# Expert layer of a two-block kernel: units in pairs, loads of half the rows of two units, gate and up products of 512 columns

## The chip, the cores and the metric

The kernel runs on one core of a Trainium2 chip. The metric is the device time of one execution in microseconds (us). Three executions of the kernel before are shown, with their median. Engines are named as the profile names them: PE is TensorE, DVE is VectorE, ACT is ScalarE, POOL is GpSimd, SP is SyncE, and PEld is PE's loading of weights.

## What is computed

The reference runs a first block of two layers (SwiGLU networks, attention with a linear recurrence, a short convolution) and a second block of two layers (a mixer each, then a dense network and a layer of experts) over 256 tokens of 1024 columns. The change touches the last part alone, the layer of 8 experts with 2 chosen per token. Every expert has a hidden width of 3584:

```python
def _swiglu(x, w_gate, w_up, w_down):
    return (jax.nn.silu(x @ w_gate) * (x @ w_up)) @ w_down

def _moe_swiglu(x, w_router, b_router, w_gate, w_up, w_down):
    logits = (x @ w_router).astype(jnp.float32) + b_router.astype(jnp.float32)
    top_vals, top_idx = lax.top_k(logits, TOP_K)
    top_w = jax.nn.softmax(top_vals, axis=-1)
    combine = jnp.sum(jax.nn.one_hot(top_idx, N_EXPERTS, dtype=jnp.float32) * top_w[..., None], axis=-2)
    out = jnp.zeros_like(x)
    for e in range(N_EXPERTS):
        out = out + combine[..., e:e + 1].astype(x.dtype) * _swiglu(x, w_gate[e], w_up[e], w_down[e])
    return out
```

## The kernel before

**Units.** All weights stream from HBM once. The gate and up weights of 128 hidden columns are one unit: 1 MB in `w_gu`, 128 rows of 8 KB, each row holding gate (8 blocks `k` of 128 columns) and then up (8 blocks). The down weights of the same 128 hidden columns are 0.5 MB in `w_d`, 128 rows of 4 KB. An expert has NF2 = 28 units, the layer 224. `N0` is the number of the layer's first unit.

**Exactness.** Every product of fp32 is made of three in the fp32r type: a value is split in hi (`wh_gu`, `wh_d`, a copy by ACT) and lo (`wl_gu`, `wl_d`, a subtraction by DVE), and `mm3` (L1719) issues hi x hi, hi x lo and lo x hi; these are the lines L1721, L1722 and L1723, whoever calls it.

**One expert.** Up to 128 tokens of an expert are gathered into slots by products with a one-hot matrix (`gather`, L2209, 16 products of 128 columns for each half), modulated by ACT (L741), and split in hi and lo (`XGH`, `XGL`, shown as mixT_hi and mixT_lo). For unit i PE runs `slot_gate_up` (L2256 on): the slots are the stationary operand, and for each of 8 blocks k the moving operand is `wh_gu[:, :, k, :]`, 128 gate columns and 128 up columns, so 24 products of 256 columns into half of a PSUM bank, `PB[:, n % 2, 0:256]`. ACT takes the silu of 128 columns (L758), DVE multiplies with the up half (L1457), PE transposes the result (`h_transpose`, L2269), ACT and DVE split it (L764, L1463), and `slot_down` issues 6 products of 512 columns into two banks in which the expert's sum grows. At an expert's end ACT evicts that sum, and PE adds it to the tokens by `scatter_previous` (L2225) some units into the next expert.

**Order.** It is written out by hand for each engine, in steps i of one unit:

- PE: gate and up of i, transpose of i - 1, down of i - 2.
- ACT: silu of i, hi of h of i - 1, hi of the gate and up weights of i + 2 (`moe_hi_gu`, L726), hi of the down weights of i (`moe_hi_d`, L733).
- DVE: gated product of i, lo of h of i - 1, lo of the down weights of i - 1 (`moe_lo_d`, L1444), lo of the gate and up weights of i + 2 (`moe_lo_gu`, L1439).
- SP: the load of gate and up weights of unit i (`load_moe_gu`, L358), then of the down weights of i - 3 (L366), into four buffers each (`RAW_GU`, `RAW_D`; two of them are shown as scratch). A load waits until DVE has made the lo of the unit four before.

hi and lo tiles have two buffers: the hi of unit n waits until PE has used unit n - 2. Two more units of gate and up weights than the layer has (`NU = START[-1] + 2`) are loaded and split at the end and not used. The steps are unrolled but for loops of four steps (`Fori`), which run twice. A second pass for an expert with more than 128 tokens stands behind a branch on the number `most_members` and is not entered with these inputs.

## Time and profile before

| | us |
|---|---|
| median of 3 runs | 2753.35 |
| lowest and highest of them | 2750.55, 2759.77 |
| profiled execution, span from the first to the last instruction | 2747.2 |
| PE busy in it | 2600.3 |
| PEld, DVE, ACT, POOL busy | 2379.0, 2165.5, 1483.6, 947.8 |
| expert layer in it, from routing to the last product | about 1680 to 2730 |

The profiled execution's time is shown by its span; the three runs were timed without a profile and lie 3 to 12 us above it. A row of the timeline gives a start, a duration, engine, line, operation, and what is written from what, by the names of tiles. Durations of matmuls overlap, since their ends are modelled: the distance of two starts is what a product costs. "Idle before" names what a wait ended with. In the tables of windows, PEclk is the granted clock of PE as a share of 2.4 GHz and the DMA share is the mean busy share of 16 DMA engines.

### The profile page before, as it was taken

Reading aid. Unit: us, or ns where it says so; the run is one execution under the profiler, and the core shown is the slowest. Engines: PE = TensorE matmul, PEld = TensorE weight load, DVE = VectorE, ACT = ScalarE, POOL = GpSimd, SP = SyncE. Lnnn points to the kernel's source line nnn. Section 1 sums busy time; section 2 is a strip of 40 time slices with the busy share of each in tenths; the row PEclk is TensorE's granted clock in tenths of the full one; section 3 lists DMA queues with packets and bytes.
Section 4 is the critical chain, followed back from the end, with each engine's and each line's share of the span. In section 5 each row is a group of like instructions: output and inputs, shape, how many; then the busy total and the mean of one; then the engine's idle time right before and its main releaser. Section 6 shows DMA issues by size and latency. Waiting matters only on the chain. (4 is left out here: it accounts for less than half of the span.)

```text
span 2747.2 us, 47482 instructions
## 1 busy us (share of the span) xinstructions
PE 2600.3 (95%) x17802; PEld 2379.0 (87%) x17802; DVE 2165.5 (79%) x2488; ACT 1483.6 (54%) x1930; POOL 947.8 (34%) x586
## 2 busy tenths in 40 slices
PE   8999899999998998888998978999999999999997
PEld 7999699999897998658998747999999999999986
DVE  5667666766787676987855997898989898989888
ACT  4337543443434334424334515777777777777765
POOL 6990089688789992126900130000000000000000
PEclk9999999999999998999999988999999999999999
DMA  8664267566566653324553415999999999999985
GB/s 309 252 237 148 103 241 256 202 250 254 191 241 229 220 183 134 115 105 164 183 184 138 164 63 192 343 350 333 352 335 349 338 347 343 347 345 346 340 320 216
DMA packets 129209, 670.58 MB, mean 244 GB/s; under 512 B 14672, under 2 KB 14992, under 8 KB 80064
## 3 DMA queue, kind: packets, MB, share of 16 engines
q1 hardware_dynamic: 111024, 604.72, 59.9%
q0 software_dynamic: 18064, 64.21, 6.9%
q8 instruction: 81, 1.33, 0.2%
q14 instruction: 40, 0.33, 0.0%
HBM read 667.82 MB, written 1.05 MB: 243 GB/s over the span
## 5 line engine op out<-in xcount | busy, mean ns | idle before, releaser
L1721 PE MATMUL work<-xT_hi,wh_gu 128*128 128x256 f32 x2088 | 593.9, 284 | 21.6 <-DVE xT_lo L985 12.0
L1722 PE MATMUL work<-xT_lo,wh_gu 128*128 128x256 f32 x2088 | 592.3, 284 | 0.0
L1723 PE MATMUL work<-xT_hi,wl_gu 128*128 128x256 f32 x2088 | 591.7, 283 | 0.0
L1721 PE MATMUL work<-wh_gu,mixT_hi 128*128 128x256 f32 x1792 | 507.5, 283 | 2.8 <-DVE wl_gu L1439 1.5
L1722 PE MATMUL work<-wl_gu,mixT_hi 128*128 128x256 f32 x1792 | 505.8, 282 | 0.0
L1723 PE MATMUL work<-wh_gu,mixT_lo 128*128 128x256 f32 x1792 | 505.5, 282 | 0.0
L857 DVE TENSOR_TENSOR wl_gu<-raw_gu,wh_gu 128x2048 fp32r<-128x2048 f32 x158 | 392.3, 2483 | 72.0 <-ACT wh_gu L395 71.5
L1721 PEld LDWEIGHTS work<-xT_hi,wh_gu 128*128 128x128 f32 x2088 | 401.3, 192 | 30.1 <-issue 21.3
L1722 PEld LDWEIGHTS work<-xT_lo,wh_gu 128*128 128x128 f32 x2088 | 401.7, 192 | 4.8
L1723 PEld LDWEIGHTS work<-xT_hi,wl_gu 128*128 128x128 f32 x2088 | 401.5, 192 | 0.0
L862 DVE TENSOR_TENSOR wl_d<-raw_d,wh_d 128x1024 fp32r<-128x1024 f32 x157 | 250.2, 1594 | 189.6 <-ACT wh_d L402 189.5
L1721 PE MATMUL acc<-wh_d,h_hi 128*128 128x512 f32 x912 | 380.4, 417 | 2.8 <-DVE wl_d L1444 2.7
L1723 PE MATMUL acc<-wh_d,h_lo 128*128 128x512 f32 x912 | 361.2, 396 | 0.0
L1722 PE MATMUL acc<-wl_d,h_hi 128*128 128x512 f32 x912 | 361.1, 396 | 0.0
L1721 PEld LDWEIGHTS work<-wh_gu,mixT_hi 128*128 128x128 f32 x1792 | 340.9, 190 | 12.5 <-DVE wl_gu L1439 1.7
L1722 PEld LDWEIGHTS work<-wl_gu,mixT_hi 128*128 128x128 f32 x1792 | 341.6, 191 | 8.8
L1723 PEld LDWEIGHTS work<-wh_gu,mixT_lo 128*128 128x128 f32 x1792 | 341.5, 191 | 0.0
L402 ACT ACTIVATE wh_d<-raw_d 128x1024 fp32r<-128x1024 f32 x157 | 166.2, 1059 | 276.1 <-PE acc L1723 276.1
L395 ACT ACTIVATE wh_gu<-raw_gu 128x2048 fp32r<-128x2048 f32 x158 | 300.7, 1903 | 25.4 <-PE acc L1723 25.0
L1652 POOL TENSOR_SCALAR scratch<-scratch,small 128x1024 f32<-128x1024 f32 x84 | 312.9, 3724 | 4.2
L1439 DVE TENSOR_TENSOR wl_gu<-raw_gu,wh_gu 128x2048 fp32r<-128x2048 f32 x113 | 259.1, 2293 | 38.0 <-ACT wh_gu L726 37.9
L1439 DVE TENSOR_TENSOR wl_gu<-scratch,wh_gu 128x2048 fp32r<-128x2048 f32 x112 | 256.6, 2291 | 25.5 <-ACT wh_gu L726 25.0
(436 smaller groups left out, 4785.6 us busy)
## 6 DMA issues: line engine op xcount, KB each, us to landing
raw_gu<-in_w_gu SPq DMA_DIRECT2D x271, 1024.0 KB, 5.2
raw_d<-in_w_d SPq DMA_DIRECT2D x269, 512.0 KB, 5.4
scratch<-in_w_gu SPq DMA_DIRECT2D x112, 1024.0 KB, 7.2
scratch<-in_w_d SPq DMA_DIRECT2D x112, 512.0 KB, 7.8
scratch<-in_w_mod POOLq DMA_DIRECT2D x96, 512.0 KB, 3.7
scratch<-in_s_b POOLq DMA_DIRECT2D x16, 256.0 KB, 2.9
rows<-in_norm_post POOLq DMA_DIRECT2D x6, 512.0 KB, 4.4
rows<-in_ln_g POOLq DMA_DIRECT2D x4, 512.0 KB, 5.5
```

What stands on the lines that cost most here:

```text
L395: act.activation(wh_gu[k][:, :, :, :].rearrange("p a k n -> p (a k n)"), raw_gu[k][:, :], ACT.Copy).then_inc(gu_hi, 1)
L402: act.activation(wh_d[k][:, :], raw_d[k][:, :], ACT.Copy).then_inc(d_hi, 1)
L857: TT(wl, raw_gu[k][:, :], wh.bitcast(F32), ALU.subtract).then_inc(gu_lo, 1)
L862: TT(wl_d[k][:, :], raw_d[k][:, :], wh_d[k][:, :].bitcast(F32), ALU.subtract).then_inc(d_lo, 1)
L1439: TT(wl, RAW_GU[k] if k > 1 else RAW_GU[k][:, :], wh.bitcast(F32), ALU.subtract).then_inc(gu_lo, 1)
L1652: link(pool.tensor_scalar(MW[n % 3], MW[n % 3], c, None, ALU.mult))
L1721: pe.matmul(out_, w[0], m[0], start=start, stop=False)
L1722: pe.matmul(out_, w[0], m[1], start=False, stop=False)
L1723: return pe.matmul(out_, w[1], m[0], start=False, stop=stop)
```

## The change

Two units 2p and 2p + 1 are a pair. Their two loads of gate and up weights no longer bring one unit each: load h brings, for both units, the blocks k of half h (4h to 4h + 3), so a row of the buffer has four pieces of 2 KB (gate of either unit, up of either unit) from four places of `w_gu`. A product then takes one block k with the gate columns of both units and the up columns of both, 512 columns in four pieces of 128, into a whole bank: 12 products per load, the first load opening the sum and the second closing it. Silu, gated product and the split of h work on 256 columns once per pair; the two transposes of a pair stand together; down of a unit comes in step i + 3 instead of i + 2, hi of its weights in step i + 1, lo in step i + 2. The two surplus units go. The unrolled part of an expert is 20 steps, the looped part 2 x 4; in the last expert ACT and DVE have no loop.

```diff
-NU = START[-1] + 2
+NU = START[-1]
...
+            pairs_gu = A["w_gu"][N0:N0 + NE * NF2].rearrange("(q u) p (g h c) -> q h p g u c", u=2, g=2, h=2)
+
+            def pieces(raw):
+                return raw.rearrange("p (g u c) -> p g u c", g=2, u=2)
...
-                sp.dma_start(RAW_GU[k] if k > 1 else RAW_GU[k][:, :], A["w_gu"][dyn + n]).then_inc(gu_landed4[k], 16)
+                sp.dma_start(pieces(RAW_GU[k] if k > 1 else RAW_GU[k][:, :]),
+                             pairs_gu[pair + i // 2, i % 2]).then_inc(gu_landed4[k], 16)
...
-            for i in range(NE * NF2, NE * NF2 + 3):
-                if i < NE * NF2 + 2:
-                    load_moe_gu(i)
-                load_moe_d(i - LATER)
+            for i in range(NE * NF2 - LATER, NE * NF2):
+                load_moe_d(i)
...
-                def step(i, at, e=0):
-
-                    silu(i, at, P)
-                    if i or e:
-                        h_hi(i - 1, at)
-                    moe_hi_gu(i + 2, at)
-                    if i == 1 and e:
+                def step(i, at, pairs, e=0, more=True):
+
+                    if i % 2:
+                        silu(i // 2, at)
+                    elif i or e:
+                        h_hi(i // 2 - 1, pairs)
+                    if more:
+                        moe_hi_gu(i + 2, at)
+                    if i == 2 and e:
                         act.wait_ge(d_used, N0 + at)
                         act.activation(YS, tile2(PA[:, 0:2, :]), ACT.Copy, scale=slot_share).then_inc(moe_s["y"], 1)
-                    moe_hi_d(i, at)
-                    if i == 2 and e:
+                    if i or e:
+                        moe_hi_d(i - 1, at)
+                    if i == 3 and e:
                         y_hi(e)
...
+                moe_hi_d(NF2 - 1, at)
+                h_hi(NPAIR - 1, pairs)
...
-                def step(i, at, e=0):
-
-                    gated(i, at, P)
-                    if i or e:
-                        h_lo(i - 1, at, PA[:, 2 + (N0 + i - 1) % 2, 0:P], P)
-                        moe_lo_d(i - 1, at)
-                    moe_lo_gu(i + 2, at)
+                def step(i, at, pairs, e=0, more=True):
+
+                    if i % 2:
+                        gated(i // 2, pairs)
+                    elif i or e:
+                        h_lo(i // 2 - 1, pairs)
+                    if i > 1 or e:
+                        moe_lo_d(i - 2, at)
+                    if more:
+                        moe_lo_gu(i + 2, at)
...
+                moe_lo_d(NF2 - 2, at)
                 moe_lo_d(NF2 - 1, at)
+                h_lo(NPAIR - 1, pairs)
...
+                def part_product(out_, xg, k, w, kk, start, stop):
+
+                    wh, wl = (x[:, :, :, :].rearrange("p g (u k) n -> p (g u) k n", u=2)[:, :, kk, :] for x in w)
+                    return mm3(out_, (XGH[xg][:, k, :], XGL[xg][:, k, :]), (wh, wl), start, stop)
+
+                def slot_gate_up(i, at, xg):
+
+                    n, half = N0 + i, i % 2
                     pe.wait_ge(gu_lo, at + (n + 1))
-                    for k in range(KD):
...
+                    for kk in range(4):
+                        last = part_product(PB[:, i // 2 % 2, :], xg, 4 * half + kk, (wh_gu[n % 2], wl_gu[n % 2]), kk,
+                                            half == 0 and kk == 0, half == 1 and kk == 3)
                     last.then_inc(gu_used, 1)
...
+                def step(i, at, pairs, e, xg):
+
+                    if i < 2:
+                        pe.wait_ge(moe_s["xg_l"], 2 * e + i + 1)
+                    slot_gate_up(i, at, xg)
+                    if i % 2 == 0 and (i or e):
+                        h_transpose(i // 2 - 1, pairs)
+                    if i == 3 and e:
+                        pe.wait_ge(moe_s["y"], e)
+                    if i >= 3 or e:
+                        slot_down(i - 3, at, pairs, i == 3, i == 2)
...
+                slot_down(NF2 - 3, at, pairs)
+                h_transpose(NPAIR - 1, pairs)
+                slot_down(NF2 - 2, at, pairs)
+                slot_down(NF2 - 1, at, pairs, stop=True)
```

The pass behind the branch is changed in the same way. Three places show how the instructions move. First PE, at the border from a unit's gate and up products (work<-...) to the transpose (acc<-const,scratch) and the down products (acc<-wh_d,...), in a step of the last expert. Before:

```order
L1721 MATMUL work<-wh_gu,mixT_hi 128x256
L1722 MATMUL work<-wl_gu,mixT_hi 128x256
L1723 MATMUL work<-wh_gu,mixT_lo 128x256
L2268 REGISTER_ALU
L2269 MATMUL acc<-const,scratch 128x128
L2274 REGISTER_ALU
L1721 MATMUL acc<-wh_d,h_hi 128x512
L1722 MATMUL acc<-wl_d,h_hi 128x512
L1723 MATMUL acc<-wh_d,h_lo 128x512
```

and with the change, in an even step:

```order
L1733 MATMUL work<-wh_gu,mixT_hi 128x512
L1734 MATMUL work<-wl_gu,mixT_hi 128x512
L1735 MATMUL work<-wh_gu,mixT_lo 128x512
L2283 REGISTER_ALU
L2285 MATMUL acc<-const,scratch 128x128 x2
L2290 REGISTER_ALU
L1733 MATMUL acc<-wh_d,h_hi 128x512
```

The three rows of a block k stand eight times in a unit before and four times in a step now; they are twice as wide, and an even step has two transposes, an odd one none. Second DVE at the end of the last expert: lo of the weights (wl_gu, wl_d), the gated product (scratch<-scratch,work) and lo of h. Before:

```order
L1457 TENSOR_TENSOR scratch<-scratch,work 128x128
L1463 TENSOR_TENSOR h_lo<-acc,h_hi 128x128
L1444 TENSOR_TENSOR wl_d<-scratch,wh_d 128x1024
L1439 TENSOR_TENSOR wl_gu<-raw_gu,wh_gu 128x2048
L1463 TENSOR_TENSOR h_lo<-acc,h_hi 128x128
L1444 TENSOR_TENSOR wl_d<-scratch,wh_d 128x1024
```

and with the change:

```order
L1473 TENSOR_TENSOR h_lo<-acc,h_hi 128x256
L1456 TENSOR_TENSOR wl_d<-raw_d,wh_d 128x1024
L1468 TENSOR_TENSOR scratch<-scratch,work 128x256
L1456 TENSOR_TENSOR wl_d<-raw_d,wh_d 128x1024
L1456 TENSOR_TENSOR wl_d<-scratch,wh_d 128x1024 x2
L1473 TENSOR_TENSOR h_lo<-acc,h_hi 128x256
```

The last wl_gu is gone, and the last h_lo, which stood ahead of the last wl_d, stands behind the last three of them. Third SP, the loads at the head of the layer's loop, with the change:

```order
L364 DMA raw_gu<-in_w_gu 128x4x512
L373 DMA raw_d<-in_w_d 128x1024
L364 DMA raw_gu<-in_w_gu 128x4x512
L373 DMA scratch<-in_w_d 128x1024
L364 DMA scratch<-in_w_gu 128x4x512
```

Their order and number per unit are as before; a row of a gate and up load, 128x2048 before, is now four runs of 512 columns.

## Rows read from the trace of the kernel before

**Rows 1.** The page: its first line and the engines' busy times.

```profile
span 2747.2 us, 47482 instructions
...
PE 2600.3 (95%) x17802; PEld 2379.0 (87%) x17802; DVE 2165.5 (79%) x2488; ACT 1483.6 (54%) x1930; POOL 947.8 (34%) x586
```

**Rows 2.** Windows over the expert layer (their columns are the first line here).

```profile
core 0: us, PE busy (x) PEld busy (x) DVE busy (x) ACT busy (x) POOL busy (x), PEclk, DMA share, GB/s
...
1965.00:2090.00 125.00, 125.00 (x890) 117.16 (x890) 111.24 (x120) 91.75 (x122) 0.00 (x0) 1.00 0.93 343
```

**Rows 3.** The chain of waits from 2000 to 2030 us, by line.

```profile
by line: PE work L1722 21.1%; PE work L1721 21.1%; PE work L1723 21.1%; PE acc L1723 10.1%; PE acc L1722 10.1%; PE acc L1721 9.2%; PE work L2209 5.9%; PE acc L2269 2.2%
```

**Rows 4.** Timeline of PE: start us, us, engine, line, operation, out<-in.

```profile
2000.10 0.28 PE L1721 MATMUL work<-wh_gu,mixT_hi 128*128 128x256 f32 x1
...
2002.85 0.28 PE L1723 MATMUL work<-wh_gu,mixT_lo 128*128 128x256 f32 x1
...
2003.31 0.39 PE L1722 MATMUL acc<-wl_d,h_hi 128*128 128x512 f32 x1
...
2004.47 0.28 PE L1721 MATMUL work<-wh_gu,mixT_hi 128*128 128x256 f32 x1
```

**Rows 5.** Pieces of the chain of waits in the mixer before: start us, us.

```profile
1648.13 0.23 PE acc L1721
...
1652.92 0.23 PE acc L1721
```

**Rows 6.** Timelines of ACT, DVE and SP's queue, one unit of the layer.

```profile
2003.16 0.28 ACT L758 ACTIVATE scratch<-work 128x128 f32<-128x128 f32 x1 [1.17 <-PE work L1723]
...
2003.49 1.92 ACT L726 ACTIVATE wh_gu<-raw_gu 128x2048 fp32r<-128x2048 f32 x1
...
2003.48 0.29 DVE L1457 TENSOR_TENSOR scratch<-scratch,work 128x128 f32<-128x128 f32 x1
...
2005.45 2.29 DVE L1439 TENSOR_TENSOR wl_gu<-raw_gu,wh_gu 128x2048 fp32r<-128x2048 f32 x1 [0.35 <-ACT wh_gu L726]
...
2003.55 0.33 SPq L358 DMA_DIRECT2D raw_gu<-in_w_gu  x1
```

**Rows 7.** Groups by form, 400 to 1000 us: count, busy us, mean ns, idle before.

```profile
L523 ACT ACTIVATE scratch<-work 128x256 f32<-128x256 f32 x54 | 20.8, 385 | 153.9 <-PE work L1723 153.9
L1070 DVE TENSOR_TENSOR scratch<-scratch,work 128x256 f32<-128x256 f32 x54 | 22.6, 419 | 33.4 <-ACT scratch L523 33.4
```

**Rows 8.** Timelines of PE and ACT at the layer's start.

```profile
1694.27 0.36 PE L1721 MATMUL work<-wh_gu,mixT_hi 128*128 128x256 f32 x1 [0.60 <-DVE mixT_lo L1432]
...
1696.66 0.39 PE L1721 MATMUL work<-wh_gu,mixT_hi 128*128 128x256 f32 x1 [0.72 <-DVE mixT_lo L1432]
...
1702.85 0.39 PE L1721 MATMUL work<-wh_gu,mixT_hi 128*128 128x256 f32 x1 [1.50 <-DVE wl_gu L1439]
...
1698.57 1.90 ACT L726 ACTIVATE wh_gu<-scratch 128x2048 fp32r<-128x2048 f32 x1
```

**Rows 9.** Timelines of PE and DVE at the layer's end.

```profile
2720.69 0.27 PE L2269 MATMUL acc<-const,scratch 128*128 128x128 f32 x1
...
2726.85 0.80 PE L1721 MATMUL acc<-wh_d,h_hi 128*128 128x512 f32 x1 [2.31 <-DVE wl_d L1444]
...
2729.14 0.63 PE L1723 MATMUL acc<-wh_d,h_lo 128*128 128x512 f32 x1
...
2725.58 1.22 DVE L1444 TENSOR_TENSOR wl_d<-scratch,wh_d 128x1024 fp32r<-128x1024 f32 x1
```

**Rows 10.** Transfers of 1658:1661, 2715:2717 and 1800:1900; waits of 1720:2700.

```profile
q1 hardware_dynamic: 172, 1.28, 100.8%
...
q1 hardware_dynamic: 130, 0.45, 55.7%
...
raw_gu<-in_w_gu SPq DMA_DIRECT2D x12, 1024.0 KB, 7.3
...
ACT wh_d L733 <- DMA raw_d<-in_w_d: 0.6, 2, 0.4
```

More of the change, by code:

```diff
@@ L265, in program @@
         late = {n: sem("late_" + n) for n in ("gu_landed", "d_landed", "sum", "scattered", "added")}
-        U1, H1 = N0 + NE * NF2, M0 + NE * NF2
+        NPAIR = NF2 // 2
+        U1, H1 = N0 + NE * NF2, M0 + NE * NPAIR
         T_OF = {"ab": 16, "mix2": 5}
@@ new lines, in moe @@
+                            for h in range(2):
+                                act.dma_start(raw_gu[h][:, :].rearrange("p (g u c) -> p g u c", g=2, u=2),
+                                              pairs_gu[pair, h]).then_inc(late["gu_landed"], 16)
+                                act.dma_start(raw_d[h][:, :], A["w_d"][q + (N0 + h)]).then_inc(late["d_landed"], 16)
+                            act.wait_ge(late["gu_landed"], q * 16 + 32)
+                            for h in range(2):
+                                act.activation(wh_gu[h][:, :, :, :].rearrange("p a k n -> p (a k n)"), raw_gu[h][:, :],
+                                               ACT.Copy).then_inc(gu_hi, 1)
@@ new lines, in moe @@
+                            act.wait_ge(late["d_landed"], q * 16 + 32)
+                            for h in range(2):
+                                act.activation(wh_d[h][:, :], raw_d[h][:, :], ACT.Copy).then_inc(d_hi, 1)
+                            act.wait_ge(gu_used, q + (U1 + 2))
+                            act.activation(SG[0], PB[:, 1, 0:S], ACT.Silu).then_inc(silu_done, 1)
+                            act.wait_ge(moe_s["hT"], pair + (NE * NPAIR + 1))
+                            act.activation(HH[0][:, :], PA[:, 2, 0:S], ACT.Copy).then_inc(moe_s["hh"], 1)
@@ L2357, in moe @@
-                            for h in range(2):
-                                v = slice(h * 512, (h + 1) * 512)
-                                last = mm3(PA[:, h, :], (HH[0][:, 0:P], HL[0][:, 0:P]), (wh_d[0][:, v], wl_d[0][:, v]),
-                                           False, False)
-                            last.then_inc(d_used, 1)
+                                last = part_product(PB[:, 1, :], 0, k, (wh_gu[k // 4], wl_gu[k // 4]), k % 4,
+                                                    k == 0, k == KD - 1)
@@ new lines, in moe @@
+                                if k % 4 == 3:
+                                    last.then_inc(gu_used, 1)
+                            pe.wait_ge(moe_s["hf"], pair + (NE * NPAIR + 1))
+                            for f in range(2):
+                                last = pe.transpose(PA[:, 2, f * P:(f + 1) * P], HF[0][:, f * P:(f + 1) * P], ident)
+                            last.then_inc(moe_s["hT"], 1)
+                            pe.wait_ge(h_ready, pair + (H1 + 1))
+                            for f in range(2):
+                                part = slice(f * P, (f + 1) * P)
+                                for h in range(2):
+                                    v = slice(h * 512, (h + 1) * 512)
+                                    last = mm3(PA[:, h, :], (HH[0][:, part], HL[0][:, part]), (wh_d[f][:, v], wl_d[f][:, v]),
+                                               False, False)
+                                last.then_inc(d_used, 1)
```

222 lines of the change are left out of this document (84 added, 138 removed).

## The prediction

> **What bounds the kernel now.** I read the page first. TensorE is busy for 95% of the span, VectorE for 79%, the others for less [rows 1]. A table of windows of 125 us over the expert layer, the part that the change touches, says how full they are there: TensorE 100%, VectorE 89%, DMA share 0.93 at 343 GB/s, granted clock 1.00, the upper level of 2.4 GHz; the row shown stands for eight alike [rows 2]. So two resources are near their end, and the change helps one and loads the other.
>
> The chain of waits of 30 us in the layer holds nothing but matmuls, 21.1% on each of the three lines of gate and up, 10% on each of the down product [rows 3]: TensorE sets the pace, nothing releases it late. The timeline gives its price list [rows 4]. The 24 gate and up products of 256 columns start from 2000.10 to 2002.85: 2.75 / 23 = **119.6 ns** each. The down products of 512 columns start from 2003.31 to 2004.47 (the next unit's first product) in five steps: **232 ns**. The transpose between them pushes the second down product from 2002.85 + 0.12 + 0.23 = 3.20 to 3.31, 0.11 us. 24 x 0.1196 + 6 x 0.232 + 0.11 = 4.37 us, and the unit does repeat after 4.37 us, from 2000.10 to 2004.47. Over the layer a unit takes more: 1.573 MB at 343 GB/s is 4.59 us, since every expert adds gathers and scatters.
>
> **Gate and up, 24 products of 256 columns to 12 of 512.** The order excerpts show it. The price is a 512-column product. Nearest is the kernel's own 512-column product with these very weight tiles moving, acc<-wh_gu,mixT_hi in the mixer before: starts at 1648.13 and 1652.92 lie 21 steps apart, 228 ns [rows 5]; the down products say 232. I take 232. Bounds: 228, and 239.2, twice today's, if four pieces of 128 columns in a row stream worse than one run of 512. A pair of units then costs 24 x 232 = 5.57 us instead of 48 x 119.6 = 5.74: 0.172 us less, times 112 pairs: **-19.3 us** (bounds -30 and 0). The weight loads halve as well; they lie beside the products (a load begins before the product ahead has ended), so nothing more is booked.
> The Trainium skill, TensorE: Matmul & The Clock Gate, section on the back-to-back issue gap, has N/2.4 + 2.5 ns between isolated products: 109.2 and 215.8 ns, so a 512-column one would save 2.6 ns and the layer 7 us. The trace has 13 and 19 ns above the columns' own time at 2.4 GHz, not 2.5 both times, so I go by the rows.
>
> **Transposes.** One of 128 columns per unit becomes two together per pair: the same number, 0.
>
> **ScalarE and VectorE.** Per pair, two silus of 128 columns become one of 256: 385 ns against 2 x 280, and the product on VectorE 419 against 2 x 290 [rows 7, 6]. Both engines get lighter by some 0.1 us per pair, and neither is the bound. What matters is when the next weights are ready. Today the silu starts 0.19 us after the last gate product's slot (2002.97), hi of the unit after next at 2003.49, its lo runs from 2005.45 to 2007.74 [rows 6], and TensorE wants it at 2004.47 + 4.37 = 2008.84: 1.1 us early. In the new even step the hi stands behind two transposes and a 256-wide h_hi: at +0.70 us instead of +0.52, lo ends at +4.98, wanted at 0.22 + 1.39 + 2.79 + 1.39 = +5.79: 0.8 us early. That cover holds in the steady state, 0. Where gathers' copies come on top (steps 17 to 19) it is used up: I allow 0.2 us in each of 7 experts, and 0.5 us once at the layer's start: **+2 us**.
>
> **Start of the layer.** Today the first unit stops in its middle, 0.72 us, for the second half of xT; its silu stands ahead of hi of unit 2, which begins at 1698.57, and unit 2 then waits 1.50 us for its lo [rows 8]. Afterwards the first unit needs only the first half: 12 x 0.232 from 1694.27 ends at 1697.06, and with no silu ahead hi can start at 1697.25: **-1.3 us**.
>
> **End of the layer.** Two surplus loads with their hi and lo go: ScalarE saves 2 x 1.9 us, VectorE 2 x 2.3 us. The last lo stands on the path today: VectorE can begin lo of the last wh_d only behind it, at 2725.58, TensorE waits 2.31 us and takes the last down product at the lower clock, from 2726.85 to 2729.14 in five steps of 0.46 [rows 9]. It ends at 2729.6, 8.8 us after the last gate slot (2720.8). The new tail, by the same durations: four down products remain instead of three, two of them ahead of the transposes (2 x 1.39, and some 0.8 of waiting for their lo); hi of the last wh_d waits until the last but two is used (+3.6), h_hi stands behind it, then VectorE has lo of wh_d (1.2) ahead of h_lo (0.4): h_lo is out at +6.5. TensorE stands still from +3.8 to +6.5, longer than the 2.31 us after which the clock is seen fallen, so both last down products run slowly, the first at 0.46, the second at 0.43 a step (1.2 GHz doubles 0.213 of columns): 5.2 us, end +11.7. **+2.9 us**.
>
> **SyncE.** A load is still one instruction, and it issues for 0.33 us out of 4.4 [rows 6]. It gets more dimensions and a base of pairs; between nothing more and four times as long, 1.3 us, it is hidden: 0.
>
> **DMA.** A load of gate and up now has four pieces of 2 KB in each of 128 rows where it had one of 8 KB: 512 packets for 128. Two clean stretches price a packet [rows 10]: 3 us of gate and up alone moved 1.28 MB, 156 packets of 8 KB, and took 100.8% of 16 x 3 us: 310 ns each. 2 us of down weights alone moved 0.45 MB, 110 packets of 4 KB, in 55.7% of 32 us: 161 ns each. So 12 ns per packet beside the bytes, and a 2 KB packet is estimated at 75 + 12 = 86.5 ns; bounds 77.5 (a quarter of 310) and 161 (all of a 4 KB packet). One unit loads 8 + 8 rows on each engine: 8 x 0.310 + 8 x 0.161 = 3.77 us now, 32 x 0.0865 + 8 x 0.161 = **4.06 us** after, against 4.28 in the steady state and 4.50 with gathers (4.37 and 4.59 less 0.086). It still fits, with 5% over. Today 0.93 x 4.59 = 4.27 us are occupied; the 0.5 above 3.77 I read as the first packets after an empty queue, since in the first of those stretches, with the queue full, every engine moved 8 KB in 310 ns, 426 GB/s in all, and that part shrinks as the queue fills. Landing takes 7.3 us [rows 10] of the 13 us between a load's issue (2003.55) and its hi, the third start of hi after 2003.49 [rows 6], and in 980 us ScalarE waited for DMA 0.6 us [rows 10]. So 0.
> The Trainium skill, DMA: Bandwidth & Descriptors, section on why small descriptors are slow, has some 3 cycles per packet beside 32-byte beats at 850 MHz: an estimate of 79 ns for 2 KB, 305 for 8 KB. With it a unit would need 3.8 us and the case be safer; the rows show 310, and none shows a 2 KB packet.
>
> **Sum.** -19.3 + 2 - 1.3 + 2.9 = -15.7 us on the profiled span of 2747.2: 2731.5. The runs shown have a median of 2753.35, 6.1 above that span, so 2737.6.
>
> **The rivals.**
> - *The queue takes part of it.* The excess of 0.5 us stays with every unit: 4.06 + 0.5 = 4.56 us against 4.50 that TensorE needs, and 4.59 now. 224 x 0.03 = 7 us are left, 2746; half the excess gives the forecast. For: the share of 0.93. Against: data lands 5 us early. Chance 0.10.
> - *The wide product is no cheaper.* Moving reads in four pieces, or an accumulation into all of a bank, cost 239 ns: -19.3 becomes 0, the rest +3.6: 2757. Half of that effect gives 2747. Against: today's 256-column product reads two pieces and is not seen to pay for it: 119.6 is 13 ns over its columns at 2.4 GHz, the long run of the down product 19 ns over. Chance 0.04, within 0.3% (8 us, about what a measurement of this kernel tells from no change).
> - *It saves a third only.* What a product takes beside its columns, 13 ns for two pieces, grows with the pieces to some 23 ns for four: 236.6 ns, 31 ns saved per unit, -7 + 3.6 = -3.4: 2750. Against: the 19 ns of the down product and the 15 of the mixer's [rows 5], though on one long run. Chance 0.03. The rule of the Trainium skill's clock page named above comes to the same 7 us.
> - *The queue becomes the bound*, the side I don't forecast. One mechanism: a 2 KB packet costs much more than its bytes. It decides from (4.50 - 1.29) / 32 = 100 ns on; (4.59 - 1.29) / 32 = 103 ns is break-even. At 110 ns a unit takes 3.52 + 1.29 = 4.81 us, 224 x 0.22 = +49 us: 2803. At the bound of 161 ns it would be +415. For: share 0.93 already, four times the packets. Against: 12 ns of cost beside the bytes in both rows. Chance 0.11.
> - *The change doesn't do what it says* (a load split into several instructions, a product into two): the order shows one load and one 512-column product, so this is inside the second rival.
>
> **Numbers.** The forecast has 0.72, its own range being 2730 to 2743; the first rival 0.10, the second and third 0.07, the fourth 0.11. 2753.35 - 8 = 2745 parts faster from same: forecast and half of the first rival are faster, 0.77; the rest of the first with the second and third make 0.12; slower 0.11. The range goes from 2730 (512-column products at 230 ns give -24.7, the tail at the upper clock +0.5 instead of +2.9) to 2752, which takes in the first and third rival and leaves out the second and fourth, 0.15.
>
> **What would show it.** Right: wide products 232 ns apart, a pair of units in 8.56 us, weight loads of TensorE halved, no TensorE wait for wl_gu or wl_d in the middle of an expert beyond some 0.2 us; packets under 8 KB four times more in the layer's loads, DMA share about 0.95; one wait near 2.7 us before the last two down products at the lower clock. Wrong: ScalarE waiting for DMA on raw_gu, landing above 12 us, TensorE waiting for wl_gu all through; or products 239 ns apart.

## The result and the profile after

| | before | after |
|---|---|---|
| median, us (runs) | 2753.69 (4) | 2729.38 (4) |
| lowest, highest | 2750.55, 2759.77 | 2728.03, 2732.71 |
| profiled span | 2747.2 | 2726.0 |
| first to last start of a gate and up product | 1026.30 | 1000.60 |
| from there to the start of the last down product | 8.57 | 10.76 |

The ratio is 0.9912, interval 0.9896 to 0.9929: 24.3 us less, where 15.7 were forecast. The median lies 0.6 us below the range given. The last two lines of the table are read from starts in the timelines; I call them the **phase** and the **end**. Phase and end together explain the layer: -25.7 + 2.2 = -23.5 us. What lies ahead of the layer (its first gather starts at 1687.4 before, 1689.8 after) has no changed instruction but the layer's first loads, and moves by several us between any two runs, up to 1684.1 and 1696.0 in the runs below. That is why the spans differ by 21.2 only, and why single medians are to be read to some 3 us, phases to some tenths.

The page after, against [rows 1]:

```profile
span 2726.0 us, 40906 instructions
...
PE 2583.2 (95%) x15114; PEld 2242.1 (82%) x15114; DVE 2144.8 (79%) x2262; ACT 1467.0 (54%) x1704; POOL 948.2 (35%) x586
```

2688 products fewer, as the diff says, and PE as full as before. The same window as [rows 2]:

```profile
1965.00:2090.00 125.00, 124.81 (x576) 101.82 (x575) 111.92 (x96) 92.92 (x96) 0.00 (x0) 1.00 0.98 352
```

TensorE is still the bound at the upper clock; the DMA share went from 0.93 to 0.98, where some 0.95 was expected. The timeline of PE against [rows 4], one run of 12 wide products and the down products ahead of it:

```profile
2007.05 0.39 PE L1733 MATMUL acc<-wh_d,h_hi 128*128 128x512 f32 x1
...
2008.44 0.39 PE L1733 MATMUL work<-wh_gu,mixT_hi 128*128 128x512 f32 x1
...
2010.94 0.39 PE L1735 MATMUL work<-wh_gu,mixT_lo 128*128 128x512 f32 x1
```

Six down steps take 1.39 us, **232 ns** each; eleven wide ones 2.50 us, **227 ns** each. Here is the gain that I did not book. Over the layer (1740 to 2680 us) wide products stand about 229.5 ns apart on the mean: 227 once a run of them has settled, and by their place 226 to 232 in the first eight or so behind a down product. A pair repeats in 8.50 us (the first wide product behind two down products starts at 2004.28, and one pair on at 2012.78), 8.56 expected, 8.73 before. In the waits from 1720 to 2700 us:

```profile
PEld work L1733 <- DVE wl_gu L1451: 3.7, 14, 0.3
...
PE work L2237 <- DVE xT_lo L1489: 1.3, 7, 0.2
```

TensorE's weight loads wait 3.7 us in 14 places, two in each of seven experts, mostly beside the product still running. Part of it reaches the products. In step 22 of the first expert:

```profile
1794.52 0.50 PE L1733 MATMUL work<-wh_gu,mixT_hi 128*128 128x512 f32 x1
1794.86 0.40 PE L1734 MATMUL work<-wl_gu,mixT_hi 128*128 128x512 f32 x1
```

The first product's step is 0.34 us there and 0.30 in step 21, where 0.23 is usual: some 0.18 us an expert, 1.3 us in all. The only other wait for weights in this window is one of 0.7 us for wl_d, at the layer's end. ACT waits for no DMA; loads land in 7.6 us, 7.3 before [rows 10].

The layer's start, PE, against [rows 8]:

```profile
1696.55 0.50 PE L1733 MATMUL work<-wh_gu,mixT_hi 128*128 128x512 f32 x1 [0.40 <-DVE mixT_lo L1444]
...
1704.14 0.50 PE L1733 MATMUL work<-wh_gu,mixT_hi 128*128 128x512 f32 x1 [1.86 <-DVE wl_gu L1451]
...
1705.85 0.63 PE L1733 MATMUL work<-wh_gu,mixT_hi 128*128 128x512 f32 x1
1706.28 0.63 PE L1734 MATMUL work<-wl_gu,mixT_hi 128*128 128x512 f32 x1
```

Unit 2 starts 7.59 us behind the first product, 8.58 before. But the wait of 1.86 us is followed, from 1705.43 on, by seven products 0.43 us apart, the lower level; [rows 8]'s 1.50 us was not. The layer's end, against [rows 9]:

```profile
2697.14 0.40 PE L1735 MATMUL work<-wh_gu,mixT_lo 128*128 128x512 f32 x1
...
2699.60 0.50 PE L1733 MATMUL acc<-wh_d,h_hi 128*128 128x512 f32 x1 [0.67 <-DVE wl_d L1456]
...
2704.16 0.48 PE L1733 MATMUL acc<-wh_d,h_hi 128*128 128x512 f32 x1 [2.67 <-DVE h_lo L1473]
...
2705.77 0.63 PE L1733 MATMUL acc<-wh_d,h_hi 128*128 128x512 f32 x1
...
2707.91 0.63 PE L1735 MATMUL acc<-wh_d,h_lo 128*128 128x512 f32 x1
```

The wait for h_lo is there as forecast (2.67 us, 2.7 expected). The clock however falls 1.3 us behind it, so the down products of one unit and not of two run at 0.43 us a step. Even that is not fixed. The run with whole rows below has the same order and the same wait:

```profile
2704.11 0.48 PE L1732 MATMUL acc<-wh_d,h_hi 128*128 128x512 f32 x1 [2.67 <-DVE h_lo L1472]
...
2706.75 0.40 PE L1734 MATMUL acc<-wh_d,h_lo 128*128 128x512 f32 x1
```

There the steps stay at 0.23 us to the last product.

### The profile page after: what moved, and what is told of

Its sections match the earlier page's. It is cut to its first block and busy times, and to the rows that moved or that the text cites. A ratio compares the mean times of both kernels' runs of the same rounds, so it can differ in the third digit from the quotient of the medians.

```text
span 2726.0 us, 40906 instructions
## 1 busy us (share of the span) xinstructions
PE 2583.2 (95%) x15114; PEld 2242.1 (82%) x15114; DVE 2144.8 (79%) x2262; ACT 1467.0 (54%) x1704; POOL 948.2 (35%) x586
## 5 line engine op out<-in xcount | busy, mean ns | idle before, releaser
L1733 PE MATMUL acc<-wh_d,h_hi 128*128 128x512 f32 x912 | 372.0, 408 | 3.6 <-DVE h_lo L1473 2.7
L874 DVE TENSOR_TENSOR wl_d<-raw_d,wh_d 128x1024 fp32r<-128x1024 f32 x157 | 232.9, 1484 | 178.9 <-ACT wh_d L407 178.9
L1733 PE MATMUL work<-wh_gu,mixT_hi 128*128 128x512 f32 x896 | 355.2, 396 | 2.7 <-DVE wl_gu L1451 2.3
L1734 PE MATMUL work<-wl_gu,mixT_hi 128*128 128x512 f32 x896 | 351.4, 392 | 0.0
L1735 PE MATMUL work<-wh_gu,mixT_lo 128*128 128x512 f32 x896 | 350.7, 391 | 0.0
L400 ACT ACTIVATE wh_gu<-raw_gu 128x2048 fp32r<-128x2048 f32 x158 | 300.8, 1904 | 25.5 <-PE acc L1735 25.5
L1664 POOL TENSOR_SCALAR scratch<-scratch,small 128x1024 f32<-128x1024 f32 x84 | 295.0, 3512 | 4.2
L528 ACT ACTIVATE scratch<-work 128x256 f32<-128x256 f32 x116 | 44.7, 385 | 333.5 <-PE work L1735 333.5
L731 ACT ACTIVATE wh_gu<-scratch 128x2048 fp32r<-128x2048 f32 x112 | 214.0, 1910 | 1.3 <-PE work L1735 1.3
L731 ACT ACTIVATE wh_gu<-raw_gu 128x2048 fp32r<-128x2048 f32 x111 | 212.1, 1911 | 0.0
```

What stands on the lines that cost most here:

```text
L400: act.activation(wh_gu[k][:, :, :, :].rearrange("p a k n -> p (a k n)"), raw_gu[k][:, :], ACT.Copy).then_inc(gu_hi, 1)
L528: act.activation(SG[n % 2], PB[:, n % 2, 0:S], ACT.Silu).then_inc(silu_done, 1)
L731: act.activation(wh_gu[n % 2][:, :, :, :].rearrange("p a k n -> p (a k n)"), RAW_GU[k] if k > 1 else RAW_GU[k][:, :], ACT.Copy).then_inc(g ...
L874: TT(wl_d[k][:, :], raw_d[k][:, :], wh_d[k][:, :].bitcast(F32), ALU.subtract).then_inc(d_lo, 1)
L1664: link(pool.tensor_scalar(MW[n % 3], MW[n % 3], c, None, ALU.mult))
L1733: pe.matmul(out_, w[0], m[0], start=start, stop=False)
```

## The experiments

| run | median, us (runs) | ratio, interval | phase | end |
|---|---|---|---|---|
| narrow products in the new order | 2749.46 (10) | 0.9986 (0.9972 to 0.9999) | 1021.40 | 10.99 |
| whole rows | 2726.10 (4) | 0.9891 (0.9873 to 0.9908) | 1000.25 | 9.66 |
| before, pieces of 2 KB | 2749.40 (10) | 0.9988 (0.9973 to 1.0003) | 1026.43 | 8.52 |
| before, no surplus units | 2746.36 (6) | 0.9970 (0.9957 to 0.9983) | 1026.48 | 5.88 |
| one run of 512 | 2727.43 (4) | 0.9896 (0.9868 to 0.9924) | 1000.27 | 10.60 |
| down from the slots | 2719.98 (4) | 0.9864 (0.9833 to 0.9895) | 993.33 | 9.61 |
| long runs | 2721.82 (4) | 0.9874 (0.9846 to 0.9902) | 997.24 | 7.34 |
| end reordered | 2726.18 (4) | 0.9892 (0.9864 to 0.9920) | 998.58 | 7.87 |
| h in the slots' tiles | 2718.14 (4) | 0.9868 (0.9846 to 0.9891) | 993.02 | 9.62 |
| pieces of 1 KB | 2730.30 (4) | 0.9904 (0.9879 to 0.9928) | 998.60 | 10.64 |
| down in pieces | 2730.35 (4) | 0.9907 (0.9884 to 0.9929) | 998.45 | 9.66 |
| long runs, h in the slots' tiles | 2714.29 (4) | 0.9854 (0.9829 to 0.9880) | 988.74 | 7.27 |
| h 32 bytes on | 2728.66 (4) | 0.9921 (0.9904 to 0.9937) | 1001.75 | 11.19 |
| h in the slots' tiles, 32 bytes on | 2726.24 (4) | 0.9913 (0.9897 to 0.9930) | 1000.27 | 9.64 |
| before, h 32 bytes on | 2756.33 (10) | 1.0019 (1.0006 to 1.0031) | 1029.88 | 8.58 |
| long runs, h 32 bytes on | 2721.37 (4) | 0.9894 (0.9878 to 0.9911) | 999.78 | 7.34 |
| before, h 96 bytes on | 2754.59 (10) | 1.0005 (0.9990 to 1.0020) | 1029.74 | 8.53 |
| long runs, h 96 bytes on | 2723.85 (4) | 0.9890 (0.9857 to 0.9923) | 1000.40 | 7.32 |

The ratios are to the kernel before in the same session, whose medians were 2751.7 to 2755.3. A phase near 998.5 where 1000.3 is to be expected is one thing, seen three times (end reordered, pieces of 1 KB, down in pieces): their clock did not fall behind the wait ahead of unit 2, and that is worth these 1.8 us. An end of 9.6 where 10.6 to 11.2 stands in other runs of the same order is the like at the other side: behind the same wait of 2.67 us the clock stayed up, in five runs (whole rows, down from the slots, h in the slots' tiles with and without the 32 bytes, down in pieces), and that is worth 1.1 us.

**The width.** The changed kernel with its products cut in two again, but for the first block of a pair, which opens the sum of a whole bank:

```diff
+                    if start:
+                        return mm3(out_, (XGH[xg][:, k, :], XGL[xg][:, k, :]), (wh, wl), start, stop)
+                    for g in range(2):
+                        last = mm3(out_[:, g * S:(g + 1) * S], (XGH[xg][:, k, :], XGL[xg][:, k, :]),
+                                   (wh[:, 2 * g:2 * g + 2, :], wl[:, 2 * g:2 * g + 2, :]), False, stop and g == 1)
+                    return last
```

> The changed kernel with its pairs, loads and order, but every 512-column gate and up product except the first block of a pair (which opens the sum) cut into two of 256 columns. The result stays the reference's. Theory 'width' (the whole gain is the spacing of products, 2 x 119.7 against 229.8 ns in the changed kernel's trace): 42 narrow for 21 wide per pair, 21 x 9.6 ns = 0.20 us x 112 = +22.6 us on the changed kernel, so about 2752 us, a ratio of 0.999 to the kernel before. Rival 'the rest' (pairing of silu and splits, surplus units, loads): it keeps most of the gain, 2730 to 2740 us, ratio 0.992 to 0.995.

PE's timeline of this run:

```profile
2005.29 0.28 PE L1733 MATMUL work<-wh_gu,mixT_hi 128*128 128x256 f32 x1
2005.40 0.28 PE L1734 MATMUL work<-wl_gu,mixT_hi 128*128 128x256 f32 x1
2005.52 0.28 PE L1735 MATMUL work<-wh_gu,mixT_lo 128*128 128x256 f32 x1
2005.64 0.28 PE L1733 MATMUL work<-wh_gu,mixT_hi 128*128 128x256 f32 x1
```

Starts are 0.12 us apart again and the phase is 20.8 us longer, 22.6 with the 1.8 us of clock that this run did not lose at its start. Loads, order and halved elementwise work of the change are all in it, and its phase is 4.9 us from the kernel before: 1.4 of them are the down products moved to the end, and 3.3 the three products of each pair that were left wide (3 x 112 x 9.9 ns). The width alone makes the gain.

**The transfers.** The change with whole rows of 8 KB, and the kernel before with pieces of 2 KB. The edit of the first (the second is its reverse in the kernel before):

```diff
-                sp.dma_start(pieces(RAW_GU[k] if k > 1 else RAW_GU[k][:, :]),
-                             pairs_gu[pair + i // 2, i % 2]).then_inc(gu_landed4[k], 16)
+                sp.dma_start(RAW_GU[k] if k > 1 else RAW_GU[k][:, :], A["w_gu"][dyn + n]).then_inc(gu_landed4[k], 16)
```

> The changed kernel, but each gate and up load brings a whole unit in rows of 8 KB as before, not half rows of two units; the products then multiply wrong blocks, all else is as in the changed kernel. Theory 'the queue is hidden': same time as the changed kernel within 2 us (2727 to 2732), DMA share back from 0.98 to about 0.94, landing not shorter by more than 0.5 us. Rival 'the queue takes part of the gain': faster than the changed kernel by 4 us or more, 2725 or less.

> The kernel before with its order and its 256-column products, but gate and up loads in four pieces of 2 KB per row, from two units; the products then multiply wrong blocks. Theory 'the queue is hidden': same as the kernel before, ratio 0.999 to 1.001, share about 0.96. Rival 'a packet of 2 KB costs time on the path': slower by 4 us or more, ratio above 1.0015.

Neither phase moves by more than 0.4 us; that the first run's median is 3 us under the change's is 1.1 us of clock at the end, and else the part ahead of the layer. Later the edge was sought with eight pieces of 1 KB a row, by `rearrange("(m a) (b d) -> (a b) m d", m=8, b=8)` of a unit's weights:

> The changed kernel, but a load of gate and up weights has eight pieces of 1 KB in each row (other columns; as many bytes). In the changed kernel a packet of 2 KB took 84 ns in a burst, and one of 8 KB 309 before: 75 ns of bytes per 2 KB and 9 beside them. Theory A (a fixed 9 ns or so beside the bytes): a 1 KB packet takes 47 ns, a unit 64 x 0.047 + 8 x 0.159 = 4.28 us of the queue, against 4.25 that TensorE needs in the steady state and 4.47 with gathers: the share rises to 0.99 or 1.00, landing times grow from 7.6 us to 10 and more, the time stays within 6 us of the changed kernel or is up to 10 us above. Rival B (a packet below 2 KB costs as much as one of 2 KB, 84 ns): a unit takes 6.6 us, the layer 224 x 2.2 = 480 us more. If the price rises to 55 ns, it is 4.79 us per unit and +75 us.

From the view of transfers, 1800 to 1900 us, the loading queue's packets, MB and share of 16 engines. With whole rows of 8 KB:

```profile
q1 hardware_dynamic: 6658, 36.44, 96.7%
```

In the changed kernel, with pieces of 2 KB:

```profile
q1 hardware_dynamic: 15356, 35.96, 98.9%
```

With pieces of 1 KB:

```profile
q1 hardware_dynamic: 27162, 36.11, 103.2%
```

In 1600 us of engine time 8698 packets more take 35 us more, and the next 11806 take 69. The MB differ a little (at the 75 ns per 2 KB of the prediction's working, 18 us less and 5 us more), so it is 53 / 8698 and 64 / 11806: **5 to 6 ns a packet** beside its bytes by the shares. By single packets it is more: from 1800 to 2600 us the median packet takes 309 ns with 8 KB, 159 with 4 KB, 84 with 2 KB and 46 with 1 KB, so 75 ns per 2 KB and **9 ns** beside them; the shares show less because packets of 8 KB take 350 ns on the mean there. I had worked out 12. Eight times the packets cost no time, and landing stays at 7.8 us, where 10 and more was expected. The share reads 1.03 there, so a share near 1 does not say that the queue is the bound; 351 GB/s are moved in all three from 1740 to 2680 us, which is what TensorE asks for. Rival "the queue becomes the bound" was far off, and so was "takes part of it".

**The surplus units.** The kernel before without its two unused loads and splits:

> The kernel before without its two surplus units (no load, hi or lo of them). The result stays the reference's. My theory: only the tail gains: the lo of the last down weights no longer stands behind a lo of 2.3 us, TensorE's last wait falls from 2.31 to about 1 us or less and the clock stays up: 2 to 3 us less, ratio 0.999. Rival (the surplus makes up the unexplained part of the gain): 6 us or more less, ratio below 0.998.

The end shortens by 2.7 us (5.88 for 8.57), and no product there runs at the lower clock. The median fell by 8, of which the phase and end show 2.5. The rest is not shown: I take it for the scatter ahead of the layer, since the kernel before with pieces of 2 KB fell by 5 in the same session with phase and end unchanged.

**The layer's end.** The change with the last transposes ahead of the third last down product, and hi and lo of the last h ahead of the last wh_d and wl_d:

```diff
+                h_transpose(NPAIR - 1, pairs)
                 slot_down(NF2 - 3, at, pairs)
-                h_transpose(NPAIR - 1, pairs)
                 slot_down(NF2 - 2, at, pairs)
```

> The changed kernel with the layer's end alone reordered: the last two transposes ahead of the third last down product, hi and lo of the last h ahead of the last unit's down weights. Theory A (the 2.67 us wait for the last h_lo and the fall of the clock that follows it are what makes the end 2.2 us longer than before): no wait above 1.5 us, the clock stays at the upper level to the last down product, last gate start to last down start 8.5 us or less instead of 10.8; time 2 to 3 us less. Rival B (the down weights' lo is what the end hangs on, whatever stands before it): the wait moves to wl_d, end unchanged within 0.5 us.

PE's timeline, the waits ahead of the last three down products:

```profile
2701.73 0.50 PE L1734 MATMUL acc<-wh_d,h_hi 128*128 128x512 f32 x1 [0.45 <-DVE wl_d L1457]
...
2703.96 0.50 PE L1734 MATMUL acc<-wh_d,h_hi 128*128 128x512 f32 x1 [0.56 <-DVE wl_d L1457]
...
2705.86 0.50 PE L1734 MATMUL acc<-wh_d,h_hi 128*128 128x512 f32 x1 [0.24 <-DVE wl_d L1457]
```

Three waits of at most 0.56 us stand for one of 2.67, the clock stays up, and the end takes 2.9 us less. Theory A holds for the order of the end. Of the 2.9 us 1.8 are the shorter waits; the other 1.1 are the clock, which stayed up behind the long wait too in five runs.

**Why 227 and not 232.** Wide and down product have the same shapes; they differ in pieces, in what their stationary operand is, and in how long a run they form. One run of 512 for the wide product, four pieces for the down product:

> The changed kernel, but the moving operand of every wide gate and up product is one run of 512 columns of the weight tile instead of four pieces of 128 (the columns are the wrong ones; number, size and order of the products stay). In the changed kernel wide gate and up products stood 229.5 ns apart on the mean, and the down products, whose moving operand is one run, 231 to 235. Theory A (the columns set the price, pieces are free): spacing stays at 227 to 230, the phase from the first to the last gate product at 1000.6 +- 1 us, time the same within 2 us. Rival B (four pieces are read faster than one run, which is why the down products are dearer and why I sized the term too small): spacing goes to 232 or more, the phase grows by 2688 x 2.5 ns = 6.7 us or more, to 1007. Rival C (pieces cost a little and one run would be cheaper still): below 227, phase below 996.

> The changed kernel, but the moving operand of the down products is four pieces of 128 columns, 1 KB apart, instead of one run of 512 (output columns in another order). Theory A (pieces are free): spacing of the down products within 1 ns of 231 to 235, first to last gate start 1000.6 +- 1 us. Rival B (a run is read worse than pieces): down products fall to 227, 1344 x 5 ns = 6 us less. Rival C (pieces cost): more than 1002.

Pieces are free: 1000.27, and 998.45 with the clock kept up, the same as the two other runs in which it was. Next the down product with a foreign, old stationary operand:

```diff
-                        last = mm3(PA[:, h, :], (HH[p % 2][:, f], HL[p % 2][:, f]),
+                        last = mm3(PA[:, h, :], (XH[:, 5 + h, 0:P], XL[:, 5 + h, 0:P]),
```

> The changed kernel, but the stationary operand of the down products is a block of the slots' own tiles, written long before, instead of h, written just before (the output is another one; products, waits and order stay). Theory A (the down product's 231 to 235 ns is what a product costs just after a switch of operands, the first ones of a run): spacing of the down products unchanged within 1 ns, time the same within 2 us. Rival B (a freshly written stationary operand costs the down product 4 ns): down products go to 227 or 228, the layer is 1344 x 4 ns = 5 us shorter.

The phase falls by 7.3 us. Down products average 227 to 231 by their place in the run, where they had 230 to 233, and the wide ones behind them 227 to 228 from the first on, where they had 226 to 232. So it is the operand, and it lingers into the products behind. Fresh or in a bad place? h itself was put into two free blocks of the slots' tiles:

```diff
+        SH, SL = ([x[:, 6 + i, :] for i in range(2)] for x in (XH, XL))
...
-                    act.activation(HH[p % 2][:, :], PA[:, 2 + p % 2, 0:S], ACT.Copy).then_inc(moe_s["hh"], 1)
+                    act.activation(SH[p % 2], PA[:, 2 + p % 2, 0:S], ACT.Copy).then_inc(moe_s["hh"], 1)
```

> The changed kernel, but h (hi and lo) is written to two free blocks of the slots' own tiles (xT_hi, xT_lo, blocks 6 and 7) instead of tiles of its own; the same values, waits and order. It parts what the run with a foreign stationary operand left together. Theory A (the place of the stationary operand sets its price): spacing of products as in that run, first to last gate start 993 to 995 us, time 2720 to 2723. Rival B (a stationary operand that was written just before is dear, wherever it lies): 1000.6 +- 1 us and 2728 to 2730, as in the changed kernel.

Theory A: 993.02, with h just as fresh. PE's timeline, six down products and twelve wide ones as above:

```profile
2007.43 0.39 PE L1734 MATMUL acc<-wh_d,xT_hi 128*128 128x512 f32 x1
...
2008.79 0.39 PE L1734 MATMUL work<-wh_gu,mixT_hi 128*128 128x512 f32 x1
...
2011.51 0.38 PE L2286 MATMUL acc<-const,scratch 128*128 128x128 f32 x2
```

Six steps in 1.36 us, then twelve in 2.72: 227 ns for both. By the addresses of the compiled program h's own tiles begin 32 bytes above a multiple of 128, the slots' blocks at a multiple. So the address's remainder was the next theory: unused bytes around h's tiles, or an offset in the slots' tiles.

```diff
+        sb("pad0", [P, 8])
         HH = [sb(f"h_hi{i}", [P, S], F32R) for i in range(2)]
         HL = [sb(f"h_lo{i}", [P, S], F32R) for i in range(2)]
+        sb("pad1", [P, 8])
```

> The changed kernel with 32 unused bytes per partition ahead of h's own four tiles and 32 behind them, so that they begin at a multiple of 64 bytes instead of 32 above one. Theory A (the remainder of the stationary operand's address sets the price): products as in the run with h in the slots' tiles, 227 ns for most; first to last gate start 993 to 995 us; some 2719 us. Rival B (the region does: h beside the constants against h in the slots' tiles): 1000.6 +- 1 and 2729, as the changed kernel. Rival C (a multiple of 128 is needed): nothing or a part of it, 997 to 1001.

> h in the slots' tiles as before, but 32 bytes further on (32 above a multiple of 128). Theory A (remainder): the down products go back to 231 to 235 ns, first to last gate start back from 993.0 to 1000 +- 1 us, about 2727 us. Rival B (region): 993 and 2718 stay.

> The kernel before with the same 2 x 32 bytes around h's tiles. Its down products stood 229 to 235 ns apart, the narrow ones behind them at 117 to 120. Theory A (remainder): down products at 227 to 228, 1344 x 5 ns = 6.5 us less in the layer, and something in the networks before it, which use the same tiles; 2742 to 2747 us. Rival B (region, or a price that shows only beside wide products): 2753 within 3 us.

The second speaks for the remainder: in the same tiles, but 32 bytes above a multiple of 128, the phase is 1000.27 again. Its edit moved h by more than 32 bytes, to columns 8 on of block 5 where the run before had block 6. But the run with the foreign operand read blocks 5 and 6 from their first columns, 32 bytes below, and had 993.33, so it is not the blocks. The count behind PE in one window of 940 us (1740 to 2680; columns as in [rows 2]) tells the same. The change:

```profile
1740.00:2680.00 940.00, 938.67 (x4322) 766.15 (x4321) 844.78 (x709) 698.59 (x713) 0.00 (x0) 1.00 0.97 351
```

h in the slots' tiles:

```profile
1740.00:2680.00 940.00, 938.09 (x4354) 772.10 (x4353) 851.08 (x714) 702.66 (x718) 0.00 (x0) 1.00 0.96 352
```

The same, 32 bytes on:

```profile
1740.00:2680.00 940.00, 938.68 (x4323) 766.39 (x4323) 845.16 (x710) 698.20 (x714) 0.00 (x0) 1.00 0.96 351
```

Of the 7.6 us 7.3 are in these steps: 3.6 us less in the 1100 steps between two down products, 3.7 less in the 2466 between two wide ones. But the own tiles at 64 above a multiple of 128 gave nothing (1001.75), and the kernel before got slower, 1.0019, its phase longer by 3.6 us. The last pair put them, 96 bytes on (`pad0` of 24 columns), at a multiple of 128:

> The kernel before with 96 unused bytes ahead of h's own tiles and 32 behind them, so that h and everything behind it begin at a multiple of 128 bytes plus what they had. Theory A (a stationary operand that doesn't begin at a multiple of 128 bytes costs a 512-wide product some 5 ns, and the ones behind it some): first to last gate start from 1026.3 to 1019 to 1022 us, time 2742 to 2748. Rival B (the price shows only with wide products before and behind, and before, 24 narrow ones of 120 ns hide it): 1026 and 2750 to 2754.

> Long runs with h's own tiles at a multiple of 128 bytes. Theory A (the remainder to 128 sets the price): first to last gate start 989 +- 1 us, 2712 to 2717 us in all, as with h in the slots' tiles at the same remainder. Rival B (the slots' tiles are better for another reason, and 32 bytes off happened to spoil it): 997 to 1000 and 2721.

No theory A: 1029.74 where 1019 to 1022 was expected, and 1000.40 in long runs where 989 was. Both are longer by over 3 us than without padding (1026.30, 997.24), which no rival had. So neither the region alone (993.0 and 1000.3 in one region) nor the remainder to 128 alone (988.7 and 1000.4 at one remainder) sets the price. The padding moved everything behind h too, the scratch tile by 128 bytes among it, so that those runs are not clean of a second cause. The steps say where it acts: in the kernel before those between down products sum to 274.8 us and with the last padding to 275.1, so h at a multiple of 128 bought them nothing; 2.4 of the 3.4 us more lie at transposes and gathers, which read scratch. And behind two transposes the steps of the next products take 228 to 236 ns with h in the slots' tiles too, so h's place is not the whole of it. **It stays open** what of the addresses matters. Shown is that where h lies is worth 7.6 us of the phase with the same instructions, and 8.5 in the long runs below.

**Long runs.** Both gate and up steps of a pair, then both down products of the pair before, on every engine, with an end in the manner of the reordered one:

```diff
+                    for u in range(2):
...
+                        slot_gate_up(2 * p + u, at, xg)
+                        if u == 0 and (p or e):
+                            h_transpose(p - 1, pairs)
...
+                    if p or e:
+                        slot_down(2 * p - 2, at, pairs, p == 1, False)
...
+                        slot_down(2 * p - 1, at, pairs, False, p == 0)
```

> The changed kernel with both gate and up steps of a pair in one run (24 wide products), then both down products of the pair before (12), instead of 12 and 6 in turn; the end of the layer is in another order too, with the last transposes and the last h ahead of the last two down weights' lo. Theory A (the first products of each run are dearer than the settled 227 ns, so half the switches save something): the period of a pair falls from 8.50 to about 8.43 us, the phase from first to last gate start by 112 x 0.06 = 7 us to about 994; the mean of wide products to 228. Rival B (a product costs the same wherever it stands): the period stays at 8.50, phase 1000.6 +- 1.5. Rival C (the longer time between a weight tile's lo and its use, and ScalarE's and VectorE's work in larger lumps, makes TensorE wait): waits for wl_gu in mid expert of over 0.3 us in every pair, phase over 1005 and the time slower. The end of the layer gives back up to 3 us of 10.8 in any of the cases.

> Long runs (24 wide products, then 12 down products) together with h in the blocks of the slots' tiles. If the place is what makes down products dear: 997.2 us from first to last gate start, less some 6 us, 991, and about 2715 us in all. If it is not: 997 and 2722, as long runs alone.

> Long runs with h's own tiles moved by 32 bytes. If the remainder is the cause: as long runs with h in the slots' tiles, first to last gate start 989 +- 1 us and 2711 to 2716 us in all, perhaps some us less, since the networks before the layer use these tiles too. If not: 997 and 2722.

Long runs give 3.4 us of the phase, half of theory A's 7, and 3.4 us of the end, 1.1 of it the clock. With h's own tiles moved by 32 bytes the phase is 999.78, worse than either forecast. With h in the slots' tiles, from 1740 to 2680 us:

```profile
1740.00:2680.00 940.00, 939.75 (x4370) 775.90 (x4371) 841.80 (x719) 706.29 (x721) 0.00 (x0) 1.00 0.95 354
```

48 products more than the change in the same time. This is the version to keep: 2714.29 us, 38 below the kernel before in its session; its phase and end together are 15.4 us shorter than the change's.

## Why the prediction came out too high

Direction, mechanism and bound were right; the size was not, and the range ended 0.6 us too high. Phase and end took 23.5 us less, 7.8 more than forecast: that is the miss, and no scatter. That the median fell outside the range is scatter: the sum behind the range's lower end is -23.5 too (-24.7 + 2 - 1.3 + 0.5), and the 0.6 us below it are less than what single medians move by. By the prediction's own steps:

- **The wide product, -19.3.** The step "The down products say 232. I take 232" failed. The nearest row had been named in the same breath: the mixer's product with these very weight tiles moving, 228 [rows 5]. Measured: about 229.5 on the mean. From the start of the ninth unit (35.5 us behind the first product before, 34.1 after) to the last product the 216 units took 990.8 us and now take 966.5: 0.225 us a pair for 0.172, **-25.2 us** over 112 pairs. The 1.3 us of waits below are inside it, so the products' own saving is 26.5 us. The runs say why the down product misled: in the step where it takes 232 ns it takes 227 with h in the slots' tiles. It had the right width, but another stationary operand in another place.
- **Allowances, +2.** Of it 0.2 us was for each of 7 experts, and that was nearly right: 0.18 us, but at steps 21 and 22 and not at 17 to 19. The 0.5 for the start is in the next term. It is counted here as 0, since the -25.2 holds it.
- **The start, -1.3.** Unit 2 came 1.0 us earlier, and hi of it began 3.10 us behind the first product, 2.98 forecast. Not seen: that the wait ahead of unit 2 would be followed by a stretch at the lower clock, 1.5 us. By the ninth unit it stands 1.35 us ahead, of which 1.4 is a down product that moved to the end and 0.9 the first pairs' products, so the start cost **+0.9**.
- **The end, +2.9.** An error of accounting: the fourth down product behind the last gate slot, 1.39 us, is not new work, it left the phase. The term should have been +1.5. Measured 10.76 - 8.57 = 2.2, less 1.4 is **+0.8**, since one unit's down products ran slowly, not two units'. That "both last down products run slowly" failed as a rule: in five runs with the same wait none did, and with their end (9.65) the term would have been -0.3.
- **Transposes, SyncE, DMA, 0.** Right. SP issues a load of four pieces for 0.62 us, 0.33 before, hidden. For DMA see the pieces.

The sum of the measured: -25.2 (the 1.3 us of waits in it) + 0.9 + 0.8 = -23.5. Had 228 been taken and the 1.4 booked once, the sum would have been -30 + 2 - 1.3 + 1.5 = -27.8, 4.3 beyond the -23.5; with the mean of both rows, 230, it would have been -24.7 + 2.2 = -22.5. The range's lower end rested on 230 ns and a tail at the upper clock; the nearest row's own 228 was a bound in the text and was left out of the range. That its sum equals the measured one is luck: its terms are -24.7, +2, -1.3 and +0.5, and the runs show -26.5, +1.3, +0.9 and +0.8 in their places.

The rule of the Trainium skill cited there (TensorE: Matmul & The Clock Gate, back-to-back issue gap) gave 2.6 ns saved by a wide product; the runs show 2 x 119.7 - 229.5 = 9.9 ns. What a product takes beside its columns at 2.4 GHz is some 13.4 ns, for 256 (120.0 settled, less 106.7) and for 512 columns (226.8 settled, less 213.3) alike. One of the two is saved: 13 ns, less what the first products of a run cost. For the packet, the Trainium skill (DMA: Bandwidth & Descriptors, why small descriptors are slow) has some 3 cycles beside the bytes, at that page's 850 MHz an estimate of 3.5 ns; the traces have 5 to 6 by the shares and 9 by single packets, so more than that and less than my 12.

## What to carry to other kernels

Where a product is the whole bound, take its price from the row that shares the most operands with it, put the next nearest row in the range too, and multiply the difference by the count before choosing: 4 ns were 11 us here. When work moves between two terms of a sum, write it with both signs. And before a rewrite, try the place of a small, often loaded stationary operand, and the order at the very end, where a wait of over 2 us can be paid twice, once as a wait and once in clock.

## What the runs showed that was not expected

- The same instructions with a stationary operand at another address take 7.6 us less of 1000: 3 ns on the mean of a step between down products, and 1.5 on the mean of one between the wide products behind them. 32 bytes off a multiple of 128 in the same tiles undo it. The rule behind it is not found.
- A DMA share of 1.02 to 1.03 with 1 KB packets cost nothing, not even landing time (7.8 us).
- A wait of 1.86 us, and one of 1.68 us in the run with the end reordered, stood at the same place of the layer's start; behind the first the clock fell, behind the second it did not. The granted clock had risen at 1695.1 in the one and at 1697.4 in the other. Behind one and the same wait of 2.67 us at the layer's end it fell in five runs and stayed up in five.
